# Windowed attention in a four-layer block: weights divided before they are turned, values held by TensorE

## The chip, the cores and the metric

One NeuronCore of a Trainium2 chip runs the whole program; the other cores are idle. The time is the device time of one launch in microseconds (us), the median of the runs shown; lower is better. Instructions of five engines run side by side: TensorE (PE, its weight loads as PEld), VectorE (DVE), ScalarE (ACT), GpSimd (POOL) and SyncE (SP, which only issues DMAs here). They are ordered among each other by semaphores alone.

## The reference

256 tokens of width 1024 pass four layers (two of differential attention, one of stick-breaking attention, one of windowed attention with sinks), each followed by a gated feed-forward network, and then a fifth block that mixes dilated attention with a state-space model. Only the windowed layer, the third, matters here. It has 16 query heads of 64 features, 2 key/value heads (8 query heads share one), a window of 128 tokens, and 2 blocks of 128 queries:

```python
qkv = h @ w_in
q, k, v = jnp.split(qkv, [nq, nq + nkv], axis=-1)
...
sc = jnp.where(mask[None, :, None, None], sc, -jnp.inf)
m = jnp.maximum(jnp.max(sc, axis=-1, keepdims=True), sink)
p = jnp.exp(sc - m)
probs = p / (jnp.sum(p, axis=-1, keepdims=True) + jnp.exp(sink - m))
o = jnp.einsum('bncgqk,bnkcd->bnqcgd', probs.astype(v.dtype), vwin)
return o.reshape(b, s, C_HEADS * C_HEAD_DIM) @ w_out
```

## The kernel before

The kernel is written engine by engine: each engine has one function per kind of layer (`window` in the blocks of ACT, DVE and PE), in which its instructions stand in the order in which they run, by hand. Nothing is reordered by a scheduler. What one engine does too late, another waits for at the place written down.

**Weights.** Matrices stream through a ring of three buffers ("units" of 1 MB, `RING` = 3). ACT rounds each unit to a head (`head`), DVE takes the rest (`rest`, original minus head), and PE makes each product of three matmuls (`product`, lines 2114 to 2116: head by head, rest by head, head by rest). A unit is loaded when the unit three before has been split by DVE, and ACT may overwrite a head only after PE has used it. The windowed layer has nine units, s = 0 to 8: five of 256 columns for the input projection (in PE's code `half_unit(s, m)` for the token half m, 24 matmuls each), and four for the output projection (`out_products`, `out_tile`, 512 columns a matmul). `rest(u + s + RING)` in DVE's order splits the unit that comes three later.

**Attention.** The 16 heads are 8 pairs t = 0 to 7. For each pair:

- PE makes the scores into PSUM (`scores`: mask, then two query blocks of two heads, 384 columns a head). Only 384 of 512 key columns are there: queries 0 to 127 see 128 keys, queries 128 to 255 see 256.
- DVE takes maxima (`peak`, ends with `m_done`), ACT the exponentials with their sums into `pr` (`exp`, ends with `e_done`), DVE adds the sink's term and takes the reciprocal (`sums`, ends with `w_done`). `pr` has queries on partitions.
- PE turns the six 128x128 blocks of exponentials, so that keys are on partitions (`weights_turned`, waits for `e_done`: the undivided exponentials are turned), ACT copies them to SBUF (`spread_out`, `t_done`).
- PE multiplies by the values (`values`): the turned block of weights is the stationary operand and 64 columns of values are streamed, three matmuls a head. The result has tokens on partitions.
- DVE divides by the denominator on the way out of PSUM, into `tok` (`heads_out`, `divided`, `o_done_v`).
- For two pairs at a time PE turns `tok` (`tok_turned`, four 128x128 blocks, `xt_ready`), ACT and DVE take head and rest of it (`xt`) as the stationary operand of the output projection.

Every true f32 matmul shows as two instructions in the trace, so `values` has 12 rows a pair. `divided` is also used by the fifth block. The stick-breaking layer has a `values` of its own (lines 2985 and 2987), in which values are held and weights streamed; its rows are used below. `pr`, the turned weights `p_t` and `sc`, and the score banks have two buffers each (pair t uses t % 2).

PE's order in the layer: `half_unit(3, 0)`, query turn 2, `half_unit(3, 1)` with the weights of pairs 0 and 1 turned before its last six matmuls, scores 2 and 3, values 0 and 1, `half_unit(4, 0)`, and so on to the output units, between which the pairs 4 to 7 are finished; then `closing_products`.

Of the kernel before, what the change touches and what calls it, by code (L numbers as in the profile page):

```python
# [28 lines left out]
ALU = mybir.AluOpType  # L29
# [3 lines left out]
P = 128  # L33
TOK = 256
# [4 lines left out]
HD = 64  # L39
# [84 lines left out]
C_XT = (6, 7, 6, 4)  # L124
# [55 lines left out]
def build(nc, a, out, layers=DEPTH):  # L180
    ctx = ExitStack()
    with ctx:
# [264 lines left out]
        O_V = 8 * layer_names.count("window")  # L447
# [89 lines left out]
        def win_o(t):  # L537

            at = 256 * (t % 2)
            return ps[:, (7, 7, 6, 3)[t // 2], at:at + 256]  # L540
# [260 lines left out]
        def _(act):  # L801
# [88 lines left out]
            def window(u):  # L890

                def turned(i):
# [36 lines left out]
                spread_out(2)  # L929
                spread_out(3)  # L930
                xt(0)
# [17 lines left out]
                n["o"] += 8  # L949
# [413 lines left out]
        def _(dve):  # L1363
# [227 lines left out]
            def dilated(u):  # L1591
# [51 lines left out]
                def gated(t):  # L1643
                    dve.wait_ge(e_done, n["pair"] + t + 1)
                    step(dve.reciprocal(rcp[:, t % 4, :], den[:, t % 2, :]))
                    dve.wait_ge(o_ready, n["o"] + t + 1)
                    divided(t, ps[:, 7, 0:256])
                    dve.wait_ge(o_done_v, O_V + t + 1)
                    w = slice(P * t, P * t + P)
                    dve.tensor_tensor(tok[:, :, w], tok[:, :, w], ga_d[:, :, w], ALU.mult).then_inc(tok_ready, 1)  # L1650
# [98 lines left out]
            def window(u):  # L1749
# [72 lines left out]
                heads_out(4)  # L1822
# [4 lines left out]
                heads_out(6)  # L1827
# [3 lines left out]
                n["o"] += 8  # L1831
# [274 lines left out]
        def _(pe):  # L2106
# [242 lines left out]
            def dilated(u):  # L2349
# [195 lines left out]
                pe.wait_ge(o_done_v, n["o_v"] + 1)  # L2545
# [8 lines left out]
                pe.wait_ge(o_done_v, n["o_v"] + 2)  # L2554
# [15 lines left out]
                pe.wait_ge(o_done_v, n["o_v"] + 3)  # L2570
# [196 lines left out]
            def window(u):  # L2767

                tr, pair, o_, o_v, xt, ev_v = (n[k] for k in ("turn", "pair", "o", "o_v", "xt", "ev_v"))
# [15 lines left out]
                def turn_group(i):  # L2785
                    pe.wait_ge(evac_v, ev_v + i + 1)
                    if i == 4:
                        pe.wait_ge(xt_rest_done, xt + 1)
                    elif i:
                        pe.wait_ge(turn_used, tr + i)  # L2790
# [21 lines left out]
                def weights_turned(t):  # L2812
                    pe.wait_ge(e_done, pair + t + 1)
                    b = t % 2
                    for c in range(2):
                        for i, run in enumerate((seg(pr, b, 1, c)[:, 0:P], seg(pr, b, 1, c)[:, P:2 * P], seg(pr, b, 0, c))):
                            last = pe.transpose(win_s(t)[:, c, P * i:P * i + P], run, ident)
                    last.then_inc(t_ready, 1)

                def values(t):  # L2820
                    pe.wait_ge(t_done, pair + t + 1)
                    if t == 2:
                        pe.wait_ge(o_done_v, o_v + 2)
# [12 lines left out]
                def tok_turned(g):  # L2836
                    pe.wait_ge(o_done_v, o_v + 2 * g + 2)
                    if g == 0:
                        pe.wait_ge(turn_used, tr + 4)
                    elif g == 3:  # L2840
                        pe.wait_ge(t_done, pair + 8)
                    for t in range(2):
                        for m in range(M):
                            k = 2 * g + t
                            last = pe.transpose(ps[:, C_XT[g], TOK * t + P * m:TOK * t + P * m + P], tok[:, m, P * k:P * k + P], ident)
                    last.then_inc(xt_ready, 1)
# [10 lines left out]
                def two_weights_turned(t):  # L2857
                    weights_turned(t)
                    weights_turned(t + 1)

                for s in range(2, 5):
                    half_unit(s, 0)
                    turn_group(0 if s == 2 else s - 1)
                    half_unit(s, 1, (lambda: turn_group(1)) if s == 2 else (lambda: two_weights_turned(2 * s - 6)))
                    if s == 4:
                        tok_turned(0)
                    if s >= 2:
                        scores(2 * s - 4)
                        scores(2 * s - 3)
                    if s >= 3:  # L2870
                        values(2 * s - 6)
                        values(2 * s - 5)
                turn_group(4)
                pe.wait_ge(rest_done, 4 * (u + 6))
# [21 lines left out]
                tok_turned(2)  # L2896
# [9 lines left out]
                tok_turned(3)  # L2906
# [3 lines left out]
                for k, by in (("turn", 5), ("pair", 8), ("o", 8), ("o_v", 8), ("ev_v", 5)):  # L2910
                    n[k] += by
# [263 lines left out]
```

## Time and profile before

| | before |
|---|---|
| median of 3 runs | 1372.46 us (1371.3 to 1372.74) |
| the profiled execution: its own time | 1373.33 us |
| its span, from first to last instruction | 1371.6 us |
| PE busy over the span | 1351.1 us (99%) |
| DVE, ACT, POOL busy | 1020.4, 791.1, 176.8 us |
| granted TensorE clock | 1.0 throughout |

The windowed layer runs from about 630 us to 716 us of the span. A busy time counts an instruction from start to end; matmuls overlap, so what a matmul costs is the distance from its start to the next start. In the timeline a row has the start, the duration (of the group, where several are merged), engine, line, operation, output and inputs, the count, and in brackets the idle time ahead of it with what ended it.

### The profile page before, as it was taken

The page shows a single profiled execution, that of the slowest core. Times are in us where ns is not written, and L with a number is a line of the kernel's source. Part 1 is how long each engine was busy: PE and PEld are TensorE (multiplying, and loading weights), DVE is VectorE, ACT ScalarE, POOL GpSimd, SP SyncE. Part 2 cuts the span into 40 slices and gives each one's busy share as a digit, 9 for nine tenths or more (in the row PEclk, how much of TensorE's full clock was granted, in tenths as well). Part 3 has the DMA queues.
Part 4 walks back from the last instruction along what each step waited for, and adds up shares of the span by engine and source line. Part 5 has one row for each costly group of instructions (what it writes and reads, how often), then busy time and mean ns, then how long its engine had stood idle before and what let it go on. Part 6 is the DMA issues. An engine that isn't in the chain of part 4 may idle for free.

```text
span 1371.6 us, 20600 instructions
## 1 busy us (share of the span) xinstructions
PE 1351.1 (99%) x6811; PEld 1107.9 (81%) x6811; DVE 1020.4 (74%) x1930; ACT 791.1 (58%) x1546; POOL 176.8 (13%) x323
## 2 busy tenths in 40 slices
PE   7999999999999999999999999999999999999998
PEld 6888888889987888889888888888888888877657
DVE  6978666669666766669776655798887777889976
ACT  6676554556555654458656444666665554674344
POOL 4100000000111000002000000001049992000000
PEclk9999999999999999999999999999999999999999
DMA  8534766675433767773336777654456666553132
GB/s 285 163 123 133 235 214 222 214 247 189 155 109 111 233 217 231 230 233 119 113 111 209 231 229 227 218 182 144 139 179 224 214 215 221 182 165 122 62 123 92
DMA packets 180309, 249.24 MB, mean 182 GB/s; under 512 B 10392, under 2 KB 124640, under 8 KB 180240
## 3 DMA queue, kind: packets, MB, share of 16 engines
q1 hardware_dynamic: 152352, 224.05, 50.4%
q10 hardware_dynamic: 25920, 18.89, 4.6%
q0 software_dynamic: 1968, 5.43, 1.4%
q8 instruction: 38, 0.62, 0.2%
q14 instruction: 31, 0.25, 0.1%
HBM read 237.84 MB, written 10.49 MB: 181 GB/s over the span
## 4 chain that ended last, share of the span: by engine, by line
PE 88%; DVE 7%; ACT 3%; issue 1%; DMA 1%; ACTq 0%; SPq 0%; DVEq 0%
PE ps L2114 22%; PE ps L2116 22%; PE ps L2115 22%; PE ps L2120 3%; PE ps L2128 3%; PE ps L2124 3%; DVE w_rest L1384 2%; ACT w_head L832 1%; PE ps L2451 1%; PE ps L2392 1%; DVE x L1447 1%; PE ps L2940 1%; PE ps L2941 1%; PE ps L2942 1%; PE ps L2144 1%
## 5 line engine op out<-in xcount | busy, mean ns | idle before, releaser
L2114 PE MATMUL ps<-w_head,xt_head 128*128 128x512 f32 (+1 forms) x1152 | 448.2, 389 | 2.7 <-DVE w_rest L1384 2.3
L2116 PE MATMUL ps<-w_head,xt_rest 128*128 128x512 f32 (+1 forms) x1152 | 441.4, 383 | 0.0
L2115 PE MATMUL ps<-w_rest,xt_head 128*128 128x512 f32 (+1 forms) x1152 | 440.9, 383 | 0.0
L832 ACT ACTIVATE w_head<-w_raw,gain_t 128x512 fp32r<-128x512 f32 (+1 forms) x596 | 375.1, 699 | 85.2 <-PE ps L2116 24.7
L1384 DVE SCALAR_TENSOR_TENSOR w_rest<-w_raw,gain_t,w_head 128x512 fp32r<-128x512 f32 (+1 forms) x596 | 417.3, 764 | 5.3 <-ACT w_head L832 4.5
L2114 PEld LDWEIGHTS ps<-w_head,xt_head 128*128 128x128 f32 x1152 | 217.2, 189 | 47.4 <-issue 3.8
L2116 PEld LDWEIGHTS ps<-w_head,xt_rest 128*128 128x128 f32 x1152 | 217.1, 188 | 42.7
L2115 PEld LDWEIGHTS ps<-w_rest,xt_head 128*128 128x128 f32 x1152 | 217.4, 189 | 40.0
L832 ACT ACTIVATE w_head<-w_raw 128x1024 fp32r<-128x1024 f32 x124 | 124.7, 1053 | 83.0 <-PE ps L2116 76.8
L1382 DVE TENSOR_TENSOR w_rest<-w_raw,w_head 128x1024 fp32r<-128x1024 f32 x124 | 146.8, 1222 | 7.0 <-ACT w_head L832 6.6
L1992 DVE SCALAR_TENSOR_TENSOR hid<-ps,rstd_x,gate_s 128x256 f32<-128x256 f32 x88 | 38.6, 480 | 119.8 <-ACT gate_s L1128 119.8
L2114 PE MATMUL ps<-w_head,ht_head 128*128 128x512 f32 x320 | 125.1, 391 | 0.5 <-DVE ht_rest L2007 0.5
L2115 PE MATMUL ps<-w_rest,ht_head 128*128 128x512 f32 x320 | 124.5, 389 | 0.0
L2116 PE MATMUL ps<-w_head,ht_rest 128*128 128x512 f32 x320 | 124.5, 389 | 0.0
L1138 ACT ACTIVATE ht_head<-k_t 128x512 fp32r<-128x512 f32 x36 | 22.7, 632 | 151.9 <-DMA k_t<-hid_way 149.5
L714 POOL DMA_DIRECT2D gain<-in_norm_gains_dram x8 | 4.5, 558 | 768.6 <-DVE tok L1439 768.6
L2007 DVE TENSOR_TENSOR ht_rest<-k_t,ht_head 128x512 fp32r<-128x512 f32 x36 | 25.1, 697 | 89.6 <-ACT ht_head L1138 89.6
L2114 PEld LDWEIGHTS ps<-w_head,ht_head 128*128 128x128 f32 x320 | 60.1, 188 | 13.7 <-DVE w_rest L1382 0.7
L2116 PEld LDWEIGHTS ps<-w_head,ht_rest 128*128 128x128 f32 x320 | 60.1, 188 | 12.4
L2115 PEld LDWEIGHTS ps<-w_rest,ht_head 128*128 128x128 f32 x320 | 60.1, 188 | 12.3
L1128 ACT ACTIVATE gate_s<-ps,rstd_x 128x256 f32<-128x256 f32 x88 | 37.0, 471 | 45.2 <-PE ps L2116 45.2
L2120 PE MATMUL ps<-w_head,xt_head 128*128 128x512 f32 x160 | 44.5, 400 | 0.0
(506 smaller groups left out, 1697.4 us busy)
## 6 DMA issues: line engine op xcount, KB each, us to landing
w_raw<-in_ffn_w_gate_dram SPq DMA_DIRECT2D x88, 512.0 KB, 4.4
w_raw<-in_ffn_w_up_dram SPq DMA_DIRECT2D x88, 512.0 KB, 5.9
w_raw<-in_ffn_w_down_dram SPq DMA_DIRECT2D x88, 512.0 KB, 6.2
w_raw<-in_a_w_in_dram SPq DMA_DIRECT2D x48, 512.0 KB, 4.9
w_raw<-in_b_w_in_dram SPq DMA_DIRECT2D x24, 512.0 KB, 4.8
w_raw<-in_w_in_dram SPq DMA_DIRECT2D x24, 512.0 KB, 4.7
hid_way<-q_t ACTq DMA_DIRECT2D x36, 256.0 KB, 2.0
k_t<-hid_way ACTq DMA_DIRECT2D x144, 64.0 KB, 4.9
```

The lines of the kernel that those rows point to most:

```text
L832: ins = act.activation(w_head[:, s, w], raw(u)[:, w], ACT.Copy, scale=1.0 if by is None else by)
L1128: last = act.activation(gate_s[:, m, :], ps[:, bank + m, 0:FCH], ACT.Silu, scale=rstd_x[:, m:m + 1])
L1382: ins = dve.tensor_tensor(w_rest[:, s, w], w_raw[:, s, w], hd, ALU.subtract)
L1384: ins = dve.scalar_tensor_tensor(w_rest[:, s, w], raw(u)[:, w], by, hd, ALU.mult, ALU.subtract)
L1992: last = dve.scalar_tensor_tensor(hid[:, :, P * m:P * m + P], up, rstd_x[:, m:m + 1], gated, ALU.mult, ALU.mult)
L2007: dve.tensor_tensor(in_order(ht_rest), arrived, in_order(ht_head).bitcast(F32), ALU.subtract).then_inc(hidt_rest, 1)
L2114: pe.matmul(out_, hd, wh, start=first, stop=False)
L2115: pe.matmul(out_, hd, wr, start=False, stop=False)
L2116: return pe.matmul(out_, rt, wh, start=False, stop=last)
L2120: return pe.matmul(out_, kmaj_tiles[0][:, t, P * m:P * m + P], w_head[:, s, off:off + width], start=first, stop=False)
L2124: return pe.matmul(out_, kmaj_tiles[0][:, t, P * m:P * m + P], w_rest[:, s, off:off + width], start=False, stop=last)
L2128: return pe.matmul(out_, kmaj_tiles[1][:, t, P * m:P * m + P], w_head[:, s, off:off + width], start=False, stop=last)
```

## The change

In the windowed layer only:

- DVE's `sums` now also multiplies the 768 exponentials of the pair by their reciprocals, in SBUF, in place, in two instructions (512 and 256 elements), before `w_done`; PE's `weights_turned` waits for `w_done` instead of `e_done`.
- `values` holds 64 columns of values and streams 256 or 128 columns of turned weights: four matmuls a pair instead of six. The result has features on partitions, in the bank from which `xt` reads.
- DVE's `heads_out` and PE's `tok_turned` are gone. `xt_ready` comes from `values` of each odd pair.
- The orders are rewritten: DVE's `rest` of some units is split around `sums`; PE's `values(0)` and `values(1)` stand around query turn 3 instead of behind `scores(3)`, and the turns of pairs 1 and 3 behind the half unit.

```diff
-C_XT = (6, 7, 6, 4)
+C_XT = (7, 7, 6, 3)
...
 ACT: window
-                        act.wait_ge(o_ready, n["o"] + t - 3)
+                        act.wait_ge(xt_ready, xt_before + t // 2 - 1)
...
                 spread_out(2)
+                xt(0)
                 spread_out(3)
-                xt(0)
...
 DVE: window
                     step(dve.tensor_tensor(den2[:, t % 2, :], den[:, t % 2, :], sink_e[:, t % 2, :], ALU.add))
-                    dve.reciprocal(rcp[:, t % 4, :], den2[:, t % 2, :]).then_inc(w_done, 1)
-                    dve.wait_ge(w_done, n["pair"] + t + 1)
-
-                def heads_out(t):
-                    dve.wait_ge(o_ready, n["o"] + t + 2)
-                    divided(t, win_o(t))
-                    divided(t + 1, win_o(t + 1))
+                    step(dve.reciprocal(rcp[:, t % 4, :], den2[:, t % 2, :]))
+                    for q, w in ((1, slice(0, 512)), (0, slice(512, 768))):
+                        e = pr[:, t % 2, w].rearrange("p (c k) -> p c k", c=2)
+                        by = rcp[:, t % 4, 2 * q:2 * q + 2].unsqueeze(2).to_broadcast([P, 2, e.shape[-1]])
+                        last = dve.tensor_tensor(e, e, by, ALU.mult)
+                    last.then_inc(w_done, 1)
...
                 peak(1)
-                rest(u + 1 + RING)
+                sums(0)
+                rest(u + 1 + RING, some=(0, 1))
+                sums(1)
+                rest(u + 1 + RING, some=(1, 4))
                 rest(u + 2 + RING)
                 chunk_out(3)
-                sums(0)
-                sums(1)
                 peak(2)
                 peak(3)
-                rest(u + 3 + RING)
-                heads_out(0)
+                sums(2)
+                rest(u + 3 + RING, some=(0, 2))
+                sums(3)
+                rest(u + 3 + RING, some=(2, 4))
+                xt(0)
                 chunk_out(4)
-                sums(2)
-                sums(3)
-                xt(0)
                 peak(4)
                 peak(5)
-                heads_out(2)
                 xt(1)
+                sums(4)
                 rest(u + 4 + RING)
-                sums(4)
                 sums(5)
...
 PE: window
                 def weights_turned(t):
-                    pe.wait_ge(e_done, pair + t + 1)
+                    pe.wait_ge(w_done, pair + t + 1)
...
-                    for c in range(2):
-                        col = 1152 + HD * (t // 4)
-                        v0, v1 = qkv[:, 0, col:col + HD], qkv[:, 1, col:col + HD]
-                        o = [win_o(t)[:, P * q + HD * c:P * q + HD * c + HD] for q in range(M)]
-                        blk = [win_p(t)[:, 384 * c + P * i:384 * c + P * i + P] for i in range(3)]
-                        pe.matmul(o[1], blk[0], v0, start=True, stop=False)
-                        pe.matmul(o[1], blk[1], v1, start=False, stop=True)
-                        last = pe.matmul(o[0], blk[2], v0, start=True, stop=True)
-                    last.then_inc(o_ready, 1)
+                    heads = [slice(HD * c, HD * c + HD) for c in range(2)]
+                    v0, v1 = (qkv[:, m, 1152 + HD * (t // 4):1152 + HD * (t // 4) + HD] for m in range(M))
+                    for c, r in enumerate(heads):
+                        pe.matmul(win_o(t)[r, :], v0, win_p(t)[:, 384 * c:384 * c + TOK], start=True, stop=False, skip_group_check=True)
+                    for c, r in enumerate(heads):
+                        last = pe.matmul(win_o(t)[r, P:TOK], v1, win_p(t)[:, 384 * c + TOK:384 * c + MAP], start=False, stop=True, skip_group_check=True)
+                    if t % 2:
+                        last.then_inc(xt_ready, 1)
...
+                half_unit(3, 0)
+                turn_group(2)
+                half_unit(3, 1, lambda: weights_turned(0))
+                weights_turned(1)
+                scores(2)
+                scores(3)
+                half_unit(4, 0)
+                values(0)
+                turn_group(3)
+                half_unit(4, 1, lambda: weights_turned(2))
+                values(1)
+                weights_turned(3)
+                scores(4)
+                scores(5)
+                values(2)
+                values(3)
                 turn_group(4)
+                pe.wait_ge(xt_rest_done, xt + 1)
                 pe.wait_ge(rest_done, 4 * (u + 6))
                 pe.wait_ge(evac_v, ev_v + 5)
                 out_products(u + 5, 0, 0, 0)
-                tok_turned(1)
                 out_products(u + 5, 0, 0, 1)
```

Further down, `heads_out(4)`, `heads_out(6)` (DVE) and `tok_turned(2)`, `tok_turned(3)` (PE) are dropped where they stood. The counters that no instruction uses any more go too.

## Rows read from the trace of the kernel before

**Rows 1.** The page: engine busy times over the span, and the last-ending chain by engine

```profile
PE 1351.1 (99%) x6811; PEld 1107.9 (81%) x6811; DVE 1020.4 (74%) x1930; ACT 791.1 (58%) x1546; POOL 176.8 (13%) x323
...
PE 88%; DVE 7%; ACT 3%; issue 1%; DMA 1%; ACTq 0%; SPq 0%; DVEq 0%
```

**Rows 2.** Busy time by stretch: length, engines with counts, granted clock, DMA share, GB/s

```profile
636.00:660.00 24.00, 23.93 (x197) 22.10 (x196) 23.42 (x65) 15.16 (x45) 0.00 (x0) 1.00 0.39 133
...
636.00:700.00 64.00, 63.40 (x454) 55.33 (x453) 46.08 (x124) 37.65 (x112) 0.00 (x0) 1.00 0.31 100
```

**Rows 3.** Groups by line, 642.4 to 698.1 us: busy us, mean ns | idle before, releaser

```profile
L886 ACT ACTIVATE pr<-ps,neg_m 128x128 f32<-128x128 f32 x16 | 5.8, 369 | 8.7 <-DVE neg_m L1774 8.7
...
L1745 DVE TENSOR_TENSOR tok<-ps,rcp 128x256 f32<-128x256 f32 x8 | 3.0, 417 | 3.4 <-PE ps L2833 3.4
...
L2845 PEld LDWEIGHTS ps<-const,tok 128*128 128x128 f32 x16 | 1.9, 140 | 0.8 <-DVE tok L1745 0.5
```

**Rows 4.** Timeline of PE: values 0 and 1, half unit, token turn, closing

```profile
652.73 0.43 PE L2831 MATMUL ps<-qkv,p_t 128*128 128x64 f32 x2
...
655.43 0.36 PE L2114 MATMUL ps<-w_head,xt_head 128*128 128x256 f32 x1
...
658.38 0.60 PE L2794 MATMUL ps<-const,qkv 128*128 128x128 f32 x4
...
663.00 0.60 PE L2845 MATMUL ps<-const,tok 128*128 128x128 f32 x4
663.36 0.59 PE L2805 MATMUL ps<-masks_r,ident_r 128*128 128x384 f32 x2
...
698.02 1.20 PE L2120 MATMUL ps<-w_head,xt_head 128*128 128x512 f32 x4
```

**Rows 5.** Timeline of PE in the stick-breaking layer: its values

```profile
395.86 0.60 PE L2985 MATMUL ps<-p_t,qkv 128*64 128x256 f32 x4
...
396.51 0.60 PE L2985 MATMUL ps<-sc,qkv 128*64 128x256 f32 x4
...
415.23 0.65 PE L2985 MATMUL ps<-p_t,qkv 128*64 128x256 f32 x4
...
416.03 0.50 PE L2114 MATMUL ps<-w_head,xt_head 128*128 128x512 f32 x1
```

**Rows 6.** Timeline of DVE: rests, chunk out, sums, peaks

```profile
645.79 3.25 DVE L1384 SCALAR_TENSOR_TENSOR w_rest<-w_raw,gain_t,w_head 128x256 fp32r<-128x256 f32 x8
648.96 2.35 DVE L1382 TENSOR_TENSOR w_rest<-w_raw,w_head 128x1024 fp32r<-128x1024 f32 x2
651.23 0.34 DVE L1510 SCALAR_TENSOR_TENSOR scr_v<-ps,rstd_x,sinb 128x128 f32<-128x128 f32 x1
...
653.62 0.42 DVE L1517 TENSOR_TENSOR qkv<-qkv,scr_v 128x256 f32<-128x256 f32 x1
653.97 0.15 DVE L1778 TENSOR_TENSOR den<-den,sink_e 128x4 f32<-128x4 f32 x1
...
654.78 0.69 DVE L1770 TENSOR_REDUCE mx<-ps 128x2 f32<-128x512 f32 x1
...
656.18 0.68 DVE L1770 TENSOR_REDUCE mx<-ps 128x2 f32<-128x512 f32 x1
```

**Rows 7.** Timeline of ACT: exponentials and sink of pair 0, query turn, spreads

```profile
644.52 0.37 ACT L886 ACTIVATE pr<-ps,neg_m 128x128 f32<-128x128 f32 x1 [1.48 <-DVE neg_m L1774]
...
646.12 0.21 ACT L908 ACTIVATE sink_e<-sink_m 128x4 f32<-128x4 f32 x1
646.21 0.61 ACT L895 ACTIVATE q_t<-ps 128x512 f32<-128x512 f32 x1
...
648.86 1.64 ACT L902 ACTIVATE p_t<-ps 128x384 f32<-128x384 f32 x4 [0.33 <-PE ps L2817]
```

**Rows 8.** Busy time in two stretches at the program's start; columns as in Rows 2

```profile
11.40:16.20 4.80, 4.80 (x11) 3.76 (x12) 4.53 (x14) 3.42 (x6) 0.00 (x0) 1.00 1.06 395
18.70:20.80 2.10, 2.10 (x10) 1.67 (x10) 1.89 (x3) 2.10 (x5) 0.00 (x0) 1.00 0.84 205
```

More of the change, by code:

```diff
@@ L539, in win_o @@
             at = 256 * (t % 2)
-            return ps[:, (7, 7, 6, 3)[t // 2], at:at + 256]
+            return ps[:, C_XT[t // 2], at:at + 256]
         def win_s(t):
@@ L890, in window @@
             def window(u):
+                xt_before = n["xt"]
                 def turned(i):
@@ L948, in window @@
                 n["pair"] += 8
-                n["o"] += 8
                 return close("window", u + 9)
@@ L1647, in gated @@
                     divided(t, ps[:, 7, 0:256])
-                    dve.wait_ge(o_done_v, O_V + t + 1)
+                    dve.wait_ge(o_done_v, t + 1)
                     w = slice(P * t, P * t + P)
@@ L1821, in window @@
                 rest(u + 5 + RING)
-                heads_out(4)
                 sums(6)
@@ L1826, in window @@
                 rest(u + 6 + RING, some=(0, 3))
-                heads_out(6)
                 xt(3)
@@ L1830, in window @@
                 n["pair"] += 8
-                n["o"] += 8
                 residual("window", u + 9)
@@ L2544, in dilated @@
                 weights_turned(1)
-                pe.wait_ge(o_done_v, n["o_v"] + 1)
+                pe.wait_ge(o_done_v, 1)
                 turn_group(gs_d, 0, 7)
@@ L2553, in dilated @@
                 project(1).then_inc(unit_used, 1)
-                pe.wait_ge(o_done_v, n["o_v"] + 2)
+                pe.wait_ge(o_done_v, 2)
                 turn_group(gs_d, 1, 7)
@@ L2569, in dilated @@
                 driven(7)
-                pe.wait_ge(o_done_v, n["o_v"] + 3)
+                pe.wait_ge(o_done_v, 3)
                 values(3)
@@ L2767, in window @@
             def window(u):
-                tr, pair, o_, o_v, xt, ev_v = (n[k] for k in ("turn", "pair", "o", "o_v", "xt", "ev_v"))
+                tr, pair, xt, ev_v = (n[k] for k in ("turn", "pair", "xt", "ev_v"))
                 i_ = MAP * MASKS.index("window")
@@ L2786, in turn_group @@
                     pe.wait_ge(evac_v, ev_v + i + 1)
-                    if i == 4:
-                        pe.wait_ge(xt_rest_done, xt + 1)
-                    elif i:
+                    if i:
                         pe.wait_ge(turn_used, tr + i)
@@ L2812, in weights_turned @@
                 def weights_turned(t):
-                    pe.wait_ge(e_done, pair + t + 1)
+                    pe.wait_ge(w_done, pair + t + 1)
                     b = t % 2
                     for c in range(2):
-                        for i, run in enumerate((seg(pr, b, 1, c)[:, 0:P], seg(pr, b, 1, c)[:, P:2 * P], seg(pr, b, 0, c))):
+                        for i, run in enumerate((seg(pr, b, 0, c), seg(pr, b, 1, c)[:, 0:P], seg(pr, b, 1, c)[:, P:2 * P])):
                             last = pe.transpose(win_s(t)[:, c, P * i:P * i + P], run, ident)
@@ L2822, in values @@
                     if t == 2:
-                        pe.wait_ge(o_done_v, o_v + 2)
+                        pe.wait_ge(xt_rest_done, xt + 1)
                     elif t == 4:
                         pe.wait_ge(turn_used, tr + 5)
-                    for c in range(2):
-                        col = 1152 + HD * (t // 4)
-                        v0, v1 = qkv[:, 0, col:col + HD], qkv[:, 1, col:col + HD]
-                        o = [win_o(t)[:, P * q + HD * c:P * q + HD * c + HD] for q in range(M)]
-                        blk = [win_p(t)[:, 384 * c + P * i:384 * c + P * i + P] for i in range(3)]
-                        pe.matmul(o[1], blk[0], v0, start=True, stop=False)
-                        pe.matmul(o[1], blk[1], v1, start=False, stop=True)
-                        last = pe.matmul(o[0], blk[2], v0, start=True, stop=True)
-                    last.then_inc(o_ready, 1)
[L2836 to L2846, printed above, removed]
+                    heads = [slice(HD * c, HD * c + HD) for c in range(2)]
[6 more added lines that the diff above has]
+                        last.then_inc(xt_ready, 1)
                 def out_tile(unit_, c, t, m):
@@ L2856, in window @@
                 half_unit(1, 1)
[L2857 to L2872, printed above, removed]
+                half_unit(2, 0)
+                turn_group(0)
+                half_unit(2, 1, lambda: turn_group(1))
+                scores(0)
+                scores(1)
+                half_unit(3, 0)
[14 more added lines that the diff above has]
+                values(3)
                 turn_group(4)
+                pe.wait_ge(xt_rest_done, xt + 1)
                 pe.wait_ge(rest_done, 4 * (u + 6))
@@ L2895, in window @@
                 last.then_inc(unit_used, 1)
-                tok_turned(2)
                 weights_turned(7)
@@ L2905, in window @@
                 out_products(u + 8, 1, 4, 0)
-                tok_turned(3)
                 out_tile(u + 8, 1, 4, 1)
@@ L2909, in window @@
                 closing_products("window", u + 7, xt, (5, 5), 0)
-                for k, by in (("turn", 5), ("pair", 8), ("o", 8), ("o_v", 8), ("ev_v", 5)):
+                for k, by in (("turn", 5), ("pair", 8), ("ev_v", 5)):
                     n[k] += by
```

1 line of the change is left out of this document (removed).

## The prediction

> **What bounds the kernel now.** I read the engine totals and the chain first [rows 1]: PE is busy for 99% of the span and carries 88% of the chain, so what matters is how PE's work and PE's waits change. The table by stretch [rows 2] says how much room the others have in the layer: from 636 to 700 us PE is busy 63.4 of 64 us, DVE 46.1, ACT 37.7. DVE's 18 free us are not spread evenly: from 636 to 660 us it is busy 23.4 of 24. The groups by line [rows 3] show who waits: DVE for the old values (3.4 us ahead of L1745) and ACT for the maxima (8.7 us), while PE hardly waits for the division (the load ahead of a token turn, 0.8 us in all). So today the division sits behind the values, off PE's path. The timelines [rows 4 to 7] give distances from start to start, with which I walk the new order.
>
> **What it takes off PE.** Values 0 and 1 take from 652.73 to 655.43, 2.70 us for two pairs [rows 4]; and the others in the same timeline a little less, 1.25 to 1.35 a pair; for eight pairs 10.5 us. In the stick-breaking layer the same product in the new form takes 0.65 us a pair inside a run of pairs (395.86 to 396.51) and 0.80 alone (415.23 to 416.03) [rows 5]. In the new order pairs 2-3 and 4-5 are together, four stand alone: with 0.02 for the switch into it, 4 x 0.82 + 4 x 0.735 = 6.2 us. Gain 4.3 (4.6 if all cost 0.65, 3.9 if a lone pair cost 0.90). Four token turns at 0.36 to 0.45 (663.00 to 663.36 [rows 4]) go: 1.6 us. PE's work falls by 5.9 us.
>
> The Trainium skill agrees with the sign: its page TensorEngine Tiling (Array Packing), section Performance Considerations, advises to swap stationary and streaming operands and tile by columns when 64 columns are streamed. The same page, section Tiling Modes, says that a change of tiling mode drains the engine; the lone pair's extra 0.15 us in rows 5 fits that, and by its rule alone the gain stays.
>
> **What it adds to DVE.** Per pair two in-place f32 multiplications, 512 and 256 elements. Not in this trace; nearest: tensor_tensor of 1024 elements, two in 2.27 us start to start (648.96 to 651.23), and of 256 elements, 0.35 us (653.62 to 653.97) [rows 6]. That is 1.02 ns an element, so 0.61 + 0.35 = 0.96 us. Bounds: 0.86 (one instruction's rate for 768) and 1.05 (three of 256). Sum and reciprocal cost 0.40 as today (two in 653.97 to 654.78). DVE holds a `sums` for 1.36 us, and its result is there 1.43 us after the start. Eight times 0.96 is 7.7 us; the eight `divided` that go are 3.0 us [rows 3]. DVE gets 4.7 us more, and now between `exp` and the turning, where PE waits for it.
>
> The skill's page VectorE: DVE Perf Modes, section The perf-mode tier table, says that an f32 tensor_tensor runs at one element a cycle in every memory. By it the two would take about what I use; it rules out the cheap multiplication of the rival below.
>
> **The walk.** Other terms: `chunk_out` 2.74 us (651.23 to 653.97), `peak` 1.40 (654.78 to 656.18), `rest` of a 256-column unit 3.17 (645.79 to 648.96), of an output unit 2.27 [rows 6]; `exp` 1.69 (644.52 to 646.21, its sums there at 646.33), spread of a pair 0.8 [rows 7]; half unit 2.95 (655.43 to 658.38) [rows 4], an output product 0.23 (10 in 2.1 us, [rows 8], a little longer). Scores (1.39 us a pair) and turns of weights (0.64) are the same in both orders; they place events but add nothing to the difference. A semaphore costs 0.05 to 0.1. The same sums over the old order bring PE to the closing products at 697.8; the row has 698.02 [rows 4], so the walk reproduces the trace within 0.2 us.
>
> In the new order, from `peak(1)`'s end at 645.79 [rows 6]:
> - DVE waits 0.6 for exp 0, does `sums(0)` until 647.7. PE turns pair 0 at 648.0 as before.
> - Quarter of the rest, `sums(1)` 648.55 to 649.9. PE is at that turn at 649.4: waits 0.6.
> - DVE has the remainder of that rest, the next one, and chunk out 3 until 657.3 (before: 654.0). PE, with its values moved, starts half unit 4 at 653.4 (before 655.4), finds chunk 3 late by 0.2.
> - Peaks 2 and 3 start 2.5 us later than before; exp 2 ends at 660.6, `sums(2)` at 662.0. PE wants that turn at 660.0: waits 2.1. Pair 3: 0.3.
> - Query turn 4 comes at 669.5 (before 668.9), chunk out 4 ends at 669.0, peaks 4 and 5 and ACT's exp 4 shift, and so the second token block's rest: PE waits 1.4 (before 0.2).
> - `sums(4)`, a whole rest, `sums(5)`: done at 679.0. PE waits 1.5 (before 0.5 for a spread).
> - `peak(7)` ends at 684.1, a whole rest comes next, and `sums(6)` ends at 687.8. PE is there at 685.4: waits 2.5.
> - ACT does exp 7 behind spread 6, so `sums(7)` ends at 693.8: PE waits 1.1.
>
> New waits together 9.7 us; the same walk has 1.2 in the old order. So 8.5 more of waits against 5.9 less of work: +2.6 us. In a wait PE also drains: the next instruction starts from an empty pipe. Of seven places I add 0.2 us in all (bounds 0 and 1.6). Sum **+2.8 us**. From the closing products on, the order is the old one and PE-bound, so I carry it to the end unchanged. The weights of the next layer I take to arrive in time: the later `rest` put loads off by 2 to 3 us, and the DMA engines are at 0.31 of their time in this stretch [rows 2]; if they did not, the last rival's price covers it.
>
> The profiled execution would go from 1373.3 to 1376.1. That execution lies 0.9 above the median of the runs, so for the median I say 1372.46 + 2.8 = 1375.3 us. A measurement of this kernel can tell about 0.2%, 2.75 us, from no change; the forecast stands on that border.
>
> The walk's sensitivity: with multiplications of 0.86 us it gives +1.9, with 1.05 +3.3; with values at 0.65 each 0.3 less. With drains at their upper bound, 1.4 more.
>
> **Rivals.**
> - *PE's gain stands* (other side). The mechanism: DVE's products are ready before PE wants them. Place: turns 2 and 6, where I put 2.1 and 2.5 us of wait. Price: -5.9 of work with the old waits, 1366.6. For it: DVE is busy only 46 of 64 us [rows 2]. Against: it is not free where it counts, 23.4 of 24 us. It decides from a pair of multiplications under 0.57 us, where the walk crosses zero; at nothing it gives -2.5. Beyond 0.2% faster, the chain peak, exp, sum would have to be shorter too. 0.07.
> - *The walk overcounts*: each wait some 0.2 us shorter, multiplications near 0.86, or part of the delay absorbed where DVE and ACT have room behind 700 us. +0 to +1.2: 1372.5 to 1373.7. For it: DVE and ACT hold 10% of the whole chain [rows 1], part of it where layers meet. Against: the old order's walk fits to 0.2. 0.14.
> - *TensorE slows behind the waits.* At the program's start 11 products took 4.8 us, 0.44 each; soon after, 10 took 2.1, 0.21 each; the granted clock reads 1.00 (2.4 GHz) for both [rows 8]. So there is a state in which products take twice as long, early, when PE had hardly worked. One such spell of 11 costs 11 x 0.22 = 2.4 us: 1377.7, two 1380. Against: waits of 2 us stand among long stretches of dense work. The skill's page TensorE: Matmul & The Clock Gate, Part 1, says an idle engine falls to half its clock; by it one or two of the waits might do so. With other waits that the walk misses: 0.19.
>
> **How the numbers follow.** Forecast, +1.2 to +4.4 (1373.7 to 1376.9): 0.60, of which half lies beyond +2.75. The likeliest is 1375.3. Slower by over 0.2%: 0.31 of the forecast and the 0.19 of the last rival, 0.50. Faster: 0.07. Same: 0.29 and 0.14, 0.43. The range 1371.8 to 1379.0 leaves out the first rival and the worst third of the last, some 0.15; it includes the walk's bounds.
>
> **What would show it.** Right: values under 0.85 us a pair and no L2845; two DVE multiplications of about 0.69 and 0.42 us each pair; waits of PE's loads at the turning (L2817 before) for DVE that add to 7 to 9 us, largest at pairs 2 and 6; closing products at about 700.8. Wrong: turning that starts without a wait at pairs 2 and 6; multiplications off 0.96 us a pair; products at 0.4 us behind a wait; or the time from the closing products to the end changed, which would mean that the delay was absorbed or grew behind the layer.

## The result and the profile after

The changed kernel takes 1375.35 us in the median of 13 executions (1374.45 to 1377.7); the kernel before, beside it, 1372.15 (1371.3 to 1372.9, 13 executions). The ratio is 1.0027, 95% interval [1.0019, 1.0035]: slower by 3.2 us, where 2.8 was forecast. The profiled execution of the changed kernel took 1376.36 us (span 1374.6). Every execution below lies within 7 us of its kernel's fastest but one of e7, which took 7691.12 us and moves that median by 0.02 us.

The page after, the rows that answer to [rows 1]:

```profile
PE 1347.8 (98%) x6763; PEld 1099.7 (80%) x6763; DVE 1024.4 (75%) x1938; ACT 790.5 (58%) x1546; POOL 177.7 (13%) x323
...
PE 82%; DVE 10%; ACT 4%; DMA 2%; issue 1%; SPq 0%; ACTq 0%; DVEq 0%
```

TensorE has less to do (1347.8 us against 1351.1), and yet the program ends later. The chain shows who took over: PE's share fell from 88% to 82%, DVE's rose from 7% to 10%. The stretches of the layer, columns as in [rows 2], and a short one that the text comes back to:

```profile
636.00:660.00 24.00, 23.35 (x187) 20.58 (x185) 22.81 (x65) 13.67 (x38) 0.00 (x0) 1.00 0.38 133
...
680.00:700.00 20.00, 17.72 (x100) 12.76 (x101) 10.75 (x25) 11.00 (x32) 0.00 (x0) 0.91 0.27 88
...
636.00:700.00 64.00, 56.70 (x391) 45.27 (x390) 49.91 (x130) 37.17 (x111) 0.00 (x0) 0.97 0.31 99
...
687.30:690.60 3.30, 3.19 (x16) 2.34 (x18) 0.05 (x1) 1.61 (x7) 0.00 (x0) 0.51 0.93 301
```

PE is busy for 56.7 of 64 us, where it was 63.4. DVE is busy for 49.9, where it was 46.1: nobody is full over the layer, and the layer is longer. The groups by line, 642.1 to 701.1 us, say what PE waits for:

```profile
L885 ACT ACTIVATE pr<-ps,neg_m 128x128 f32<-128x128 f32 x16 | 5.8, 376 | 8.7 <-DVE neg_m L1774 8.7
...
L2811 PEld LDWEIGHTS ps<-const,pr 128*128 128x128 f32 x48 | 5.7, 150 | 7.8 <-DVE pr L1783 7.7
L1783 DVE TENSOR_TENSOR pr<-pr,rcp 128x512 f32<-128x512 f32 x8 | 5.5, 692 | 0.3
...
L1783 DVE TENSOR_TENSOR pr<-pr,rcp 128x256 f32<-128x256 f32 x8 | 3.3, 417 | 0.0
```

The turning of weights (L2811) now has 7.8 us of idle ahead of it, ended by the new multiplications (L1783), where [rows 3] had 0.8 us ahead of a token turn. The multiplications are 692 and 417 ns, as forecast (0.69 and 0.42). On PE's timeline each of these waits stands at its place:

```profile
649.75 0.88 PE L2811 MATMUL ps<-const,pr 128*128 128x128 f32 x6 [0.47 <-DVE pr L1783]
...
661.86 0.88 PE L2811 MATMUL ps<-const,pr 128*128 128x128 f32 x6 [1.92 <-DVE pr L1783]
...
667.75 0.65 PE L2823 MATMUL ps<-sc,qkv 128*64 128x256 f32 x4
...
668.45 0.60 PE L2823 MATMUL ps<-sc,qkv 128*64 128x256 f32 x4
...
673.76 0.50 PE L2110 MATMUL ps<-w_head,xt_head 128*128 128x512 f32 x1 [1.15 <-DVE xt_rest L1789]
...
678.72 0.87 PE L2811 MATMUL ps<-const,pr 128*128 128x128 f32 x6 [1.27 <-DVE pr L1783]
...
687.41 1.54 PE L2811 MATMUL ps<-const,pr 128*128 128x128 f32 x6 [2.28 <-DVE pr L1783]
688.88 1.12 PE L2823 MATMUL ps<-p_t,qkv 128*64 128x256 f32 x4
...
701.05 1.08 PE L2116 MATMUL ps<-w_head,xt_head 128*128 128x512 f32 x4
```

These are pairs 1 and 2, values 2 and 3 (0.70 us for the first, against 1.35 in the old form), the second token block, pairs 5 and 6, and the closing products (L2116), which stood at 698.02 in [rows 4]. The idle times printed here are 7.1 us. Two more things are to be seen at 687.41: the six transposes of this turn take 1.47 us until the next row starts, where those of pair 2 take 0.63, and the granted clock of 687.3 to 690.6 is 0.51, about the lower of the two levels (1.2 GHz), behind 2.28 us in which PE did nothing.

DVE's timeline shows why pair 6 is the worst:

```profile
682.25 0.69 DVE L1770 TENSOR_REDUCE mx<-ps 128x2 f32<-128x512 f32 x1
...
683.66 2.35 DVE L1382 TENSOR_TENSOR w_rest<-w_raw,w_head 128x1024 fp32r<-128x1024 f32 x2
685.93 0.15 DVE L1778 TENSOR_TENSOR den<-den,sink_e 128x4 f32<-128x4 f32 x1
686.12 0.18 DVE L1779 RECIPROCAL rcp<-den 128x4 f32<-128x4 f32 x1
686.33 1.02 DVE L1783 TENSOR_TENSOR pr<-pr,rcp 128x512 f32<-128x512 f32 x2
```

PE is at the turn of pair 6 at about 685.1. The exponentials are there at 684.2, but a whole rest (683.66 to 685.93) runs first, and the division takes until 687.35.

### The profile page after: what moved, and what is told of

It reads as the page before. It is cut to its first block, busy times and chain, and to the rows that moved or that the text cites. A ratio compares the mean times of both kernels' runs of the same rounds, so it can differ in the third digit from the quotient of the medians.

```text
span 1374.6 us, 20502 instructions
## 1 busy us (share of the span) xinstructions
PE 1347.8 (98%) x6763; PEld 1099.7 (80%) x6763; DVE 1024.4 (75%) x1938; ACT 790.5 (58%) x1546; POOL 177.7 (13%) x323
## 4 chain that ended last, share of the span: by engine, by line
PE 82%; DVE 10%; ACT 4%; DMA 2%; issue 1%; SPq 0%; ACTq 0%; DVEq 0%
PE ps L2110 20%; PE ps L2112 20%; PE ps L2111 20%; DVE w_rest L1384 3%; PE ps L2116 3%; PE ps L2124 3%; PE ps L2120 3%; ACT w_head L831 2%; PE ps L2388 1%; PE ps L2447 1%; PE ps L2140 1%; PE ps L2924 1%; PE ps L2925 1%; PE ps L2926 1%; DVE x L1447 1%
## 5 line engine op out<-in xcount | busy, mean ns | idle before, releaser
L2111 PEld LDWEIGHTS ps<-w_rest,ht_head 128*128 128x128 f32 x320 | 60.1, 188 | 12.3
L2116 PE MATMUL ps<-w_head,xt_head 128*128 128x512 f32 x160 | 44.5, 400 | 0.0
```

Of the source, the lines that this page charges most:

```text
L2111: pe.matmul(out_, hd, wr, start=False, stop=False)
L2116: return pe.matmul(out_, kmaj_tiles[0][:, t, P * m:P * m + P], w_head[:, s, off:off + width], start=first, stop=False)
```

## The experiments

Theory A, my own: the division on DVE stands between exponentials and turning, and in this written order DVE comes to it late; the waits eat more than TensorE saves. It makes a number for every edit by the walk of the prediction. Theory B: something else costs, such as the new form of `values`, DVE's load as such, or effects outside the layer. Theory C concerns the stretch at half clock alone: that the idle time brings it.

Each kernel below is the changed kernel with one edit. Differences are taken to the median of the kernel before in the same comparison (1371.92 for e1 to e4, 1372.40 for e5 to e8, 1372.32 for e9 to e12). Each median is of 11 executions, of five for e3, e4, e6 and e8. The last column is what the walk gave beforehand; for the changed kernel it leaves out the 0.2 us for draining.

| run | median, us | to before | ratio, 95% interval | walk |
|---|---|---|---|---|
| changed, first time | 1375.35 | +3.2 | 1.0027 [1.0019, 1.0035] | +2.6 |
| e1 no multiplication | 1369.05 | -2.9 | 0.9979 [0.9970, 0.9988] | -2.5 |
| e2 multiplied aside | 1370.69 | -1.2 | 0.9992 [0.9983, 1.0001] | -2.0 |
| e3 multiplied twice | 1384.19 | +12.3 | 1.0090 [1.0077, 1.0104] | +10.3 |
| e4 weights held | 1377.94 | +6.0 | 1.0039 [1.0025, 1.0053] | +4.0 |
| e5 filled wait | 1374.88 | +2.5 | 1.0020 [1.0011, 1.0029] | |
| e6 reordered | 1367.91 | -4.5 | 0.9964 [0.9950, 0.9977] | -5.6 |
| e7 by scalar | 1375.31 | +2.9 | 1.0023 [1.0014, 1.0032] | +0.9 or +4.1 |
| e8 reordered, by scalar | 1367.18 | -5.2 | 0.9963 [0.9949, 0.9976] | -6.0 |
| e9 one rest later | 1374.54 | +2.2 | 1.0016 [1.0007, 1.0025] | +2.1 |
| e10 last pairs first | 1372.04 | -0.3 | 0.9999 [0.9990, 1.0008] | 0.0 |
| e11 reordered, weights held | 1370.52 | -1.8 | 0.9985 [0.9976, 0.9994] | -1.2 |
| e12 changed, again | 1375.48 | +3.2 | 1.0023 [1.0014, 1.0032] | +2.6 |

**e1, the multiplications left out**

```diff
-                    step(dve.reciprocal(rcp[:, t % 4, :], den2[:, t % 2, :]))
-                    for q, w in ((1, slice(0, 512)), (0, slice(512, 768))):
...
-                    last.then_inc(w_done, 1)
+                    dve.reciprocal(rcp[:, t % 4, :], den2[:, t % 2, :]).then_inc(w_done, 1)
```

> Leaves out the division of the weights (sum and reciprocal stay, and w_done comes from the reciprocal); everything else is the changed kernel. Theory A (the products on DVE stand in the path of the turnings): the walk with 0 in place of 0.96 us a pair gives 2.5 us less than before, 1369.6, and PE's loads wait for DVE at the turnings for about 2.8 us instead of 13.6. Theory B (what costs is the new form of values, or something outside the windowed layer): the time stays near the changed kernel's, 1374 to 1376. Without waits beyond 2 us the granted clock should read 1.00.

1369.05 us. The waits of this kernel:

```profile
PEld ps L2806 <- DVE rcp L1779: 2.8, 4, 1.6
```

As theory A has it: the division costs 6.1 us of the changed kernel (from +3.2 to -2.9), and the new form of values without the division would be a gain. Of theory B the new form of values falls as the cause of the loss. Where the expectation says 13.6 us of waits for DVE, it adds PE's and PEld's rows of the same waits (5.9 and 7.7 us); the loads' own are 7.7.

**e2, the same load on DVE, without the link**

```diff
+                        aside = mix.rearrange("p a b -> p (a b)")[:, w].rearrange("p (c k) -> p c k", c=2)
-                        last = dve.tensor_tensor(e, e, by, ALU.mult)
+                        last = dve.tensor_tensor(aside, e, by, ALU.mult)
...
 weights_turned
-                    pe.wait_ge(w_done, pair + t + 1)
+                    pe.wait_ge(e_done, pair + t + 1)
```

> DVE does the same two multiplications of a pair, but writes the products to a tile that nobody reads, and the turnings wait for the exponentials (e_done) and turn them undivided, so the division is left out of the result. DVE's load is that of the changed kernel, only the link product to turning is cut. Theory A splits its cost: DVE's occupancy alone (peaks and chunks later) against the link. The walk gives 2.0 us less than before, 1370.2. If the link does not matter and only DVE's load does, the time stays at 1374 to 1376.

1370.69 us. Of the division's 6.1 us, 1.6 lie between e1 and e2 and 4.4 between e2 and the changed kernel. The split is not a clean one: e2 also frees the turning from the sum and the reciprocal, for which the loads of e1 still wait 2.8 us. So DVE's load alone costs 1.6 us or more, and the link from product to turning 4.4 or less. By these numbers most of the cost still lies in the link; how much of it sum and reciprocal would carry alone was not measured. The walk gave 0.8 us less time than was measured here.

**e3, the multiplications twice**

```diff
+                        aside = mix.rearrange("p a b -> p (a b)")[:, w].rearrange("p (c k) -> p c k", c=2)
+                        dve.tensor_tensor(aside, e, by, ALU.mult)
                         last = dve.tensor_tensor(e, e, by, ALU.mult)
```

> The multiplications are made twice (once into a tile that nobody reads, then in place): 1.92 us a pair on DVE instead of 0.96. Theory A, the walk: 10.3 us more than before, 1382.4, that is 7.7 more than the changed kernel, all eight extra 0.96 us counting in full, because DVE is on the path at every pair; longer waits may also halve TensorE's clock more often and add 1 to 4 us. Theory B (DVE has room, 50 of 64 us busy): most of the 7.7 us is hidden, under 1379.

1384.19 us, 9.1 more than the changed kernel (12.3 less 3.2) for 7.7 us of DVE work. That most of it would be hidden is refuted: PE's loads wait 14.0 us for the product, where it was 7.7. That each of the eight pairs counts in full is not shown, since part of the 9.1 us is the clock: TensorE ran at half clock behind three waits (2.85, 3.16 and 3.20 us), in 664 to 668, 685 to 689 and 695 to 699 us, and the changed kernel behind one. Two of the stretches:

```profile
660.00:680.00 20.00, 16.24 (x103) 12.80 (x103) 17.46 (x48) 12.71 (x46) 0.00 (x0) 0.91 0.22 74
680.00:700.00 20.00, 13.64 (x72) 9.80 (x71) 11.61 (x26) 8.33 (x27) 0.00 (x0) 0.83 0.34 105
```

**e4, the old form of values in the new order**

```diff
-                        pe.matmul(win_o(t)[r, :], v0, win_p(t)[:, 384 * c:384 * c + TOK], start=True, stop=False, skip_group_check=True)
...
+                        pe.matmul(o[1], blk[1], v0, start=True, stop=False)
+                        pe.matmul(o[1], blk[2], v1, start=False, stop=True)
+                        last = pe.matmul(o[0], blk[0], v0, start=True, stop=True)
```

> The values product goes back to its old form (turned weights held, 64 columns of values streamed, six matmuls a pair) in the order of the changed kernel, into the same banks; the layout of its result is that of the old form and the token turns are left out, so the output projection reads wrong numbers. TensorE does about 4.2 us more. Theory A: most of that fills waits; the walk gives 4.0 us more than before, 1376.2 (and up to 1.4 more with a clock drop), that is only 1.3 more than the changed kernel without such a drop. If TensorE's work set the time, it would be 4.2 more than the changed kernel, about 1379.5.

1377.94 us, 2.8 more than the changed kernel: neither the 1.3 of the walk nor the 4.2 of a TensorE that sets the time. The five executions spread from 1374.96 to 1379.78, and the mean granted clock goes with them: 1.000 for the two fastest, 0.996 for the slowest. The fastest are 3.0 and 4.1 over before, about the walk's 4.0. In the profiled execution the granted clock is 0.50 from 688.4 to 694.6 us, 6.2 us long and behind a wait of 2.24. With the clock mixed in, this run does not decide between them; e11 asks the same in another way.

**e5, the wait at pair 6 filled**

```diff
+                pe.wait_ge(e_done, pair + 7)
+                for _ in range(18):
+                    pe.transpose(win_s(6)[:, 0, 0:P], ident, ident)
                 weights_turned(6)
```

> TensorE turns the identity 18 times (2.0 us) into a free score bank where the changed kernel waits 2.3 us for the product of pair 6. Theory C (the half-speed stretch at 687.3 to 690.6 us, granted clock 0.50, comes from that idle time): the granted clock of this stretch reads 1.00, the turn of pair 6 takes 0.66 us instead of 1.47, and the time falls by 0.7 to 1.4 us against the changed kernel, to about 1374.2. Rival: the slow stretch has another cause (the DMA burst at 687 to 691, the earlier waits); then clock and time stay as they are, 1375.4.

1374.88 us, 2.5 over before. PE's timeline of it:

```profile
685.21 2.13 PE L2877 MATMUL ps<-const 128*128 128x128 f32 x18
687.66 0.87 PE L2811 MATMUL ps<-const,pr 128*128 128x128 f32 x6 [0.31 <-DVE pr L1783]
```

The turn of pair 6 is back at its normal pace, and the granted clock of 680 to 700 us is 1.00. The wait for the product of pair 7, 1.1 us in the walk, is there now (0.83 us at 693.76). The rival of the expectation, the DMA burst, falls: with the wait filled the DMA engines are as busy (0.89 of their time from 687.3 to 690.6, against 0.93), and e3's first slow stretch, 664 to 668, has no DMA traffic at all.

In time it is worth less than expected: the interval overlaps that of the changed kernel, and of its 11 executions six still read a mean clock of 0.998 or 0.999, so drops at other waits are likely, though no trace shows one. The drop itself comes again in each other profile with a wait of 2.2 to 2.3 us at pair 6: in e4, e7, e9 and e12 the clock is 0.50 for 3 us or more from about 688. In e12 it sets in 0.8 us after the turn started, so that the turn is still fast and the values behind it take 1.34 us instead of 0.70:

```profile
687.05 0.88 PE L2811 MATMUL ps<-const,pr 128*128 128x128 f32 x6 [2.29 <-DVE pr L1783]
687.85 1.12 PE L2823 MATMUL ps<-p_t,qkv 128*64 128x256 f32 x4
...
689.19 1.07 PE L2823 MATMUL ps<-p_t,qkv 128*64 128x256 f32 x4
...
700.55 1.07 PE L2116 MATMUL ps<-w_head,xt_head 128*128 128x512 f32 x4
```

What the drop costs is read against e5. From the turn of pair 0 to the closing products it is 53.3 us in the profile after (647.75 to 701.05), 53.2 in e12 (647.32 to 700.55) and 52.7 in e5 (647.92 to 700.63): 0.5 to 0.6 us. The slow stretch made PE late for pair 7, and so used up the wait that e5 has there.

**e6, the same instructions in another order**

```diff
 DVE
-                sums(0)
                 rest(u + 1 + RING, some=(0, 1))
+                sums(0)
                 sums(1)
                 rest(u + 1 + RING, some=(1, 4))
-                rest(u + 2 + RING)
-                chunk_out(3)
                 peak(2)
+                chunk_out(3)
                 peak(3)
                 sums(2)
-                rest(u + 3 + RING, some=(0, 2))
+                rest(u + 2 + RING, some=(0, 2))
                 sums(3)
-                rest(u + 3 + RING, some=(2, 4))
-                xt(0)
                 chunk_out(4)
+                xt(0)
+                rest(u + 2 + RING, some=(2, 4))
                 peak(4)
                 peak(5)
                 xt(1)
                 sums(4)
-                rest(u + 4 + RING)
+                rest(u + 3 + RING, some=(0, 2))
                 sums(5)
+                rest(u + 3 + RING, some=(2, 4))
+                rest(u + 4 + RING, some=(0, 2))
                 peak(6)
                 peak(7)
-                rest(u + 5 + RING)
                 sums(6)
-                xt(2)
+                rest(u + 4 + RING, some=(2, 4))
+                rest(u + 5 + RING, some=(0, 2))
                 sums(7)
+                rest(u + 5 + RING, some=(2, 4))
+                xt(2)
 ACT: exp(1) ahead of turned(2), exp(3) ahead of turned(3), spread_out(3) ahead of xt(0),
      xt(1) ahead of exp(4), exp(7) ahead of spread_out(6)
```

> Same instructions as the changed kernel, but DVE's rests are put behind sums and peaks where PE needs them late, and ACT does exp 1 before query turn 2, exp 3 before query turn 3, spread 3 before token block 0, and exp 7 before spread 6. Theory A: the 0.96 us a pair fit into DVE's free time if the order lets them; the walk gives 5.6 us less than before, 1366.6, with PE waiting under 2 us at the turnings, and a granted clock of 1.00. Rival: DVE's load and its data path are what costs, the order moves the waits elsewhere: 1371 to 1375.

1367.91 us, ratio 0.9964 [0.9950, 0.9977]: faster than both kernels. Its stretches, its one wait for a product, and its closing products:

```profile
636.00:660.00 24.00, 23.93 (x195) 21.43 (x193) 23.28 (x70) 16.75 (x51) 0.00 (x0) 1.00 0.26 90
...
636.00:700.00 64.00, 62.97 (x432) 51.55 (x430) 55.05 (x145) 41.21 (x120) 0.00 (x0) 1.00 0.36 116
```

```profile
PEld ps L2814 <- DVE pr L1783: 1.0, 1, 1.0
```

```profile
692.87 1.08 PE L2119 MATMUL ps<-w_head,xt_head 128*128 128x512 f32 x4
```

PE is busy 63.0 of 64 us again, now with less work to do, and DVE 55.1. The closing products come 5.2 us earlier than in [rows 4], the walk said 5.6. (The profiled execution took 1372.76 us as a whole; it lost its time between 1000 and 1100 us, where PE was busy 95.2 us and in e8 99.6, in a layer that is the same in all kernels here. PE waited there 4.45 us for an operand of the second product, and ACT, which makes it, up to 11.0 us for a DMA; in e8 the longest such wait of ACT is 6.4 us. Why that DMA was late is not known. The other four took 1366.64 to 1368.32.)

**e7 and e8, the multiplication by a scalar operand**

```diff
-                    for q, w in ((1, slice(0, 512)), (0, slice(512, 768))):
...
+                    for q in (1, 0):
+                        for c in range(2):
+                            e = seg(pr, t % 2, q, c)
+                            last = dve.tensor_scalar(e, e, rcp[:, t % 4, 2 * q + c:2 * q + c + 1], None, ALU.mult)
```

> The multiplications of a pair as four tensor_scalar instructions (256, 256, 128, 128 elements) with the reciprocal as an operand per partition, in the changed kernel's order. The skill's page VectorE: DVE Perf Modes gives f32 tensor_scalar in SBUF two elements a cycle: then about 0.7 us a pair, and the walk gives 0.9 more than before, 1373.1. If it runs at one element a cycle, it is 1.14 us a pair (four starts) and the walk gives 4.1 more than before, 1376.2.

```profile
646.24 1.01 DVE L1783 TENSOR_SCALAR pr<-pr,rcp 128x256 f32<-128x256 f32 x4
647.16 0.88 DVE L1384 SCALAR_TENSOR_TENSOR w_rest<-w_raw,gain_t,w_head 128x256 fp32r<-128x256 f32 x2
```

Four instructions hold DVE for 0.92 us (646.24 to 647.16), two tensor_tensor for 0.94. An instruction of 256 elements takes 0.35 us against 0.42, but there are four. So the time stays: 1375.31 us, +2.9, between the two numbers expected.

> The order of e6 with the multiplications of e7. Walk: about 6.0 less than before, 1366.2, since little wait is left for a cheaper multiplication to remove; 0 to 0.5 less than e6.

1367.18 us, -5.2. Against e6 (-4.5) the intervals overlap almost wholly; it counts as the same.

**e9 and e10, one end of the order at a time**

```diff
 e9, DVE
-                rest(u + 2 + RING)
                 chunk_out(3)
                 peak(2)
                 peak(3)
+                rest(u + 2 + RING)
 e10, DVE
-                rest(u + 5 + RING)
                 sums(6)
+                rest(u + 5 + RING)
 e10, ACT
+                exp(7)
                 spread_out(6)
-                exp(7)
```

> The changed kernel with one rest of DVE (the 2.3 us of the first output unit) behind peak 3 instead of ahead of chunk out 3. Theory A, the walk: chunk 3 and peaks 2 and 3 come 2.3 us earlier, the wait at pair 2 goes, but what follows (pairs 5, 6, 7) takes most of it back: 2.1 more than before, 0.6 less than the changed kernel's 2.6. If each wait were a cost of its own, the 2.1 us of pair 2 would come off: about 0.6 more than before.

1374.54 us, +2.2. The time is the walk's, one detail of the expectation is not: the wait at pair 2 does not go, it falls from 1.92 to 1.45 us. That of pair 6 stays at 2.29.

> The changed kernel with sums 6 ahead of the last whole rest on DVE, and exp 7 ahead of spread 6 on ACT. Theory A, the walk: the waits at pairs 6 and 7 are the last ones, nothing takes them back: 0.0 against before, 2.7 less than the changed kernel, plus the clock drop (0.91 in 680 to 700 us) that the 2.3 us of idle brought, up to 1.4. Rival (waits only move): as the changed kernel, 3 more than before.

1372.04 us, -0.3 [-0.10%, +0.08%]: 3.4 less than the changed kernel by one rest and one exponential moved. PE's wait at pair 6 is 0.59 us instead of 2.28, the clock of 680 to 700 us reads 1.00:

```profile
685.50 0.87 PE L2811 MATMUL ps<-const,pr 128*128 128x128 f32 x6 [0.59 <-DVE pr L1783]
```

Removing 2.3 us of DVE's work from ahead of an early pair gave 1.0 us, from ahead of the last ones 3.4. Behind the early one there are other waits that take the gain back. The two edits are not quite alike: e10 also moves an exponential, and about 0.6 of its 3.4 us is the clock drop that goes with the wait.

**e11, the old form of values in the order of e6**

> The new order of e6 with values in their old form (turned weights held, six matmuls a pair, old layout of the result, no token turns; the output projection reads wrong numbers). Beside e6 it prices the form of values alone where TensorE is not waiting: the walk gives 1.2 less than before, 4.4 more than e6. In the changed kernel's order the same swap was worth 1.3 by the walk.

1370.52 us, -1.8. Against e6, the form of values is worth 2.7 us where TensorE does not wait (3.4 against e8); its closing products stand at 696.44 against 692.87, 3.6 us later. The walk said 4.4. So most of the saving is real. Whether it is worth less in the changed kernel's order is not shown: there the same swap measured 2.8 us (e4), with the clock mixed in. e11 has the old form of values and no token turns, and it lies 1.8 us under the kernel before, close to the 1.6 us of token turns that it does without; so by this run the new order hides the multiplications and gains nothing beyond that.

**e12, the changed kernel again**

> The changed kernel unaltered, for comparison on the same chip as e9 to e11: 3.2 more than before, as measured.

1375.48 us, +3.2: the result stands.

## Why the prediction was right

*What it takes off PE.* Values of a pair inside a run: 0.70 and 0.75 us start to start (667.75, 668.45, 669.20), forecast 0.735. Alone, forecast 0.82: 0.80 for pairs 6 and 7 (in e5, 694.56 to 695.36), 0.92 and 0.96 for pairs 0 and 1, where the next instruction is late too (656.22 to 657.14, 663.38 to 664.34). Right but for some 0.2 us. That the saving is worth something is shown by e11 against e6, 2.7 to 3.6 us of the 4.3 forecast. One bound was summed wrongly: if all eight pairs cost 0.65, the gain is 10.5 - 5.2 = 5.3 us and not 4.6, and the walk moves by 1.0 and not by 0.3. The forecast did not use it.

*What it adds to DVE.* 0.94 us a pair (646.48 to 647.42) against 0.96. Right, and the other form that was tried (e7) is no cheaper. The Trainium skill's page VectorE: DVE Perf Modes, section The perf-mode tier table, says one element a cycle for this instruction, with 2293 ns for 2048 elements, 1.12 ns each. The trace agrees: 512 and 256 elements in 692 and 417 ns, 1.07 ns for each element between them.

*The walk.* It starts 0.3 us later than the profile after, so its times are to be read less 0.3. The turns: 650.0 forecast and 649.75 measured, 662.1 and 661.86 for pair 2, 679.1 and 678.72 for pair 5, 687.9 and 687.41 for pair 6. The waits: 0.6, 2.1, 1.4, 1.5, 2.5 forecast; 0.47, 1.92, 1.15, 1.27, 2.28 measured, each 0.1 to 0.25 shorter, since the printed idle ends with the last matmul's modelled end. All are where the prediction put them. Pair 7's 1.1 us is not there in the profile, because the slow stretch ahead of it took its place; in e5, without that stretch, it is there with 0.83 us. So what the forecast had left out took the place of one of its waits and added only 0.5 to 0.6 us beyond it; that the sum came this near is in part luck.

*The drain, +0.2.* Not measured by itself. The closing products came 3.3 us later than before (701.05 against 698.02, with a start 0.3 us earlier), the walk said 2.6. e12, measured from its turn of pair 0, has the same within 0.1 us, and e5, without the clock drop, 2.7. What is left between +2.8 and +3.2 is within the interval.

*The rivals.* The rival that PE's gain stands: not so, 7.7 us of waits for the product at the turnings. It decides where the prediction said, by the multiplication's price: at nothing -2.9 was measured, -2.5 forecast, still short of the 5.9 of work saved. The rival that TensorE slows behind the waits: this happens (granted clock 0.51 for 3.3 us in the profile after, 0.83 to 0.91 in two stretches of e3). Slow products behind a wait were among the signs that would show the forecast wrong, and this sign did come: the forecast's mechanism and this rival's are both at work. I gave it 0.19 together with other misses, too little as to whether it occurs, too much as to its price. I had taken the price from the program's start, where products are slow while the granted clock reads 1.00 [rows 8]; here it reads 0.51, so the two need not be the same state. It was 0.5 to 0.6 us at the closing products of the changed kernel, against the 2.4 named. The mean granted clock is 0.998 or 0.999 in 12 of the 13 executions, and in all 11 of e12; of the 75 executions of the kernel before that stand beside e1 to e12, 68 read 1.000. So it belongs in the forecast itself as a small term; with it the sum is +3.1 to +3.4.

*Carried to the end unchanged.* Closing products +3.0 us on the span's clock, the program's span +3.0 (1374.6 against 1371.6). Right.

## What to carry to other kernels

Ask of each piece of work that is moved whether someone waits for its product at its new place: the same 7.5 us of multiplications cost 1.6 us or more as mere load and up to 4.4 as a link between exponentials and turning, and with the rests that stood ahead of them moved behind, the kernel that has them is faster than the one that leaves them out in the written order (-4.5 against -2.9). When a change relieves the engine that sets the time and loads another one, write the order of the other one anew, starting from the last waits of the layer, since nothing behind them takes the gain back: moving one rest and one exponential at the end gave 3.4 us (about 0.6 of it the clock), one rest near the start 1.0. A walk over the written order with start-to-start distances of the trace before, first tried on the old order, foretold seven of the nine edits that have one number to within 1.1 us; the two misses of 2.0 (e3, e4) are those whose granted clock was lowest.

## What was not expected of the hardware

- TensorE's granted clock fell to 0.5 behind a wait of 2.28 us that followed four shorter ones, for about 3 us, and again behind waits of 2.25 to 2.29 us at the same place in e7, e9 and e12. With 18 transposes in the gap (e5), or with a wait of 0.59 us (e10), it stayed at 1.00. The Trainium skill's page TensorE: Matmul & The Clock Gate, Part 1, has idleness as the cause, and e5 and e10 agree.
- A drop behind a wait can cost less than it lasts: 3.3 us at half clock moved the closing products by 0.5 to 0.6 us, because PE was going to wait again (0.83 us, seen in e5).
- An f32 tensor_scalar of 256 elements in SBUF takes 351 ns, not much less than the 417 of tensor_tensor; one of 128 takes 282. The Trainium skill's page VectorE: DVE Perf Modes, section The perf-mode tier table, gives the former two elements a cycle, twice the rate of tensor_tensor. The trace agrees, with 0.54 ns for each element between the two sizes against 1.07. But 0.21 us of each instruction does not depend on the count (351 less 256 x 0.54), and at this size that part is the larger.
